# Norms on token columns, spread by products into PSUM, in a two-block kernel on one core

## What is computed

```python
def rmsnorm(x, g):
    xf = x.astype(jnp.float32)
    y = xf * lax.rsqrt(jnp.mean(xf * xf, axis=-1, keepdims=True) + NORM_EPS)
    return (y * g.astype(jnp.float32)).astype(x.dtype)

x = rmsnorm(x + y, final_g)                        # end of the first block
h = _rmsnorm(x, norm_mix_g) ; proj = h @ w_in      # start of the second
x = x + _mixer(...)
h = _rmsnorm(x, norm_ffn_g) ; u = h @ w_up         # FFN
x = x + _conv_ffn(...)
return _rmsnorm(x, norm_final_g)
```

## Time and profile before

| | us |
|---|---|
| median of 3 runs | 1647.12 (1646.19 to 1648.33) |
| the profiled execution | 1644.95 |
| its span | 1643.2 |
| TensorE busy | 1486.6 (90%) |
| VectorE busy | 1161.7 (71%) |
| ScalarE busy | 509.6 (31%) |
| POOL busy | 491.7 (30%) |

### The profile page before, as it was taken

How to read it: one execution, slowest core, us unless ns; L and a number is a source line. 1 busy time by engine, 2 the same in 40 slices (tenths; PEclk the granted TensorE clock), 3 DMA queues, 4 the chain that set the end, 5 groups by cost and what they waited for, 6 DMA issues and landing times.

```text
span 1643.2 us, 17617 instructions
## 1 busy us (share of the span) xinstructions
PE 1486.6 (90%) x7056; PEld 1171.9 (71%) x7056; DVE 1161.7 (71%) x1392; ACT 509.6 (31%) x670; POOL 491.7 (30%) x131
## 2 busy tenths in 40 slices
PE   6999778567998989999998888998997999999997
PEld 5778444357776868778887666776875888888885
DVE  3569988865485776679999999866245888886123
ACT  5432355411343433221221112332213333332221
POOL 0004011100143533234444233343342444344440
PEclk9999978875899999999999898999998999999999
DMA  6222000100022322223232222222332333332221
GB/s 184 81 85 77 1 1 1 51 1 28 26 89 91 103 79 84 69 78 94 86 103 77 77 77 77 77 77 77 103 98 56 96 84 102 103 103 96 77 84 51
DMA packets 163666, 123.44 MB, mean 75 GB/s; under 512 B 9115, under 2 KB 161474, under 8 KB 163586
## 3 DMA queue, kind: packets, MB, share of 16 engines
q1 hardware_dynamic: 163490, 122.19, 24.4%
q10 hardware_dynamic: 96, 0.13, 0.0%
HBM read 120.21 MB, written 2.10 MB: 74 GB/s over the span
## 4 chain that ended last, share of the span: by engine, by line
PE 63%; DVE 32%; ACT 2%; issue 2%; DMA 0%; SPq 0%; DVEq 0%; ACTq 0%
PE bank L399 17%; PE bank L400 17%; PE bank L401 17%; DVE conv_b L1929 10%; DVE op_hi L1472 2%; PE bank L552 2%; PE bank L359 2%; DVE score L1592 1%; DVE misc L1591 1%; DVE tmp L1483 1%; DVE x_res L1899 1%; PE bank L807 1%; PE bank L823 1%; DVE rs L1697 1%; DVE op_lo L1473 1%
## 5 line engine op out<-in xcount | busy, mean ns | idle before, releaser
L1008 POOL TENSOR_TENSOR w_lo<-w_raw,w_hi 128x2048 fp32r<-128x2048 f32 (+1 forms) x102 | 471.4, 4622 | 856.9 <-ACT w_hi L1055 828.8
L399 PE MATMUL bank<-op_hi,w_hi 128*128 128x512 f32 x1384 | 553.9, 400 | 50.8 <-issue 17.8
L400 PE MATMUL bank<-op_lo,w_hi 128*128 128x512 f32 x1384 | 546.8, 395 | 0.0
L401 PE MATMUL bank<-op_hi,w_lo 128*128 128x512 f32 x1384 | 546.1, 395 | 0.0
L399 PEld LDWEIGHTS bank<-op_hi,w_hi 128*128 128x128 f32 x1384 | 264.5, 191 | 117.2 <-issue 41.7
L400 PEld LDWEIGHTS bank<-op_lo,w_hi 128*128 128x128 f32 x1384 | 264.6, 191 | 57.2 <-issue 1.7
L401 PEld LDWEIGHTS bank<-op_hi,w_lo 128*128 128x128 f32 x1384 | 264.0, 191 | 57.5
L1055 ACT ACTIVATE w_hi<-w_raw 128x2048 fp32r<-128x2048 f32 (+1 forms) x111 | 210.4, 1895 | 263.6 <-PE bank L401 263.6
L1929 DVE SCALAR_TENSOR_TENSOR conv_b<-pad_b,par,conv_b 128x512 f32<-128x512 f32 x240 | 266.4, 1110 | 8.0
L2093 DVE TENSOR_TENSOR tmp<-tmp,conv_f 128x512 f32<-128x512 f32 x22 | 101.5, 4616 | 16.0 <-ACT tmp L1420 16.0
L1872 DVE TENSOR_TENSOR x_res<-bank,x_res 128x512 f32<-128x512 f32 x24 | 16.5, 688 | 123.6 <-PE bank L401 123.6
(11 more groups left out here) (362 smaller groups left out, 1864.5 us busy)
## 6 DMA issues: line engine op xcount, KB each, us to landing
w_raw<-in_w_in SPq DMA_DIRECT2D x31, 1024.0 KB, 5.0
w_raw<-in_w_up SPq DMA_DIRECT2D x44, 512.0 KB, 5.0
w_raw<-in_w_in SPq DMA_DIRECT2D x33, 512.0 KB, 5.1
w_raw<-in_w_kv SPq DMA_DIRECT2D x8, 1024.0 KB, 5.7
w_raw<-in_w_down SPq DMA_DIRECT2D x8, 1024.0 KB, 5.1
w_raw<-in_w_out SPq DMA_DIRECT2D x4, 1024.0 KB, 5.1
w_raw<-in_w_att_out SPq DMA_DIRECT2D x4, 1024.0 KB, 5.0
w_raw<-in_w_a_out SPq DMA_DIRECT2D x4, 1024.0 KB, 5.0
```

The source lines that it names most:

```text
L399: nc.tensor.matmul(b[:, 0:width], h, xh[:, x0 + k, 0:width], start=start and k == ks[0], stop=False)
L400: nc.tensor.matmul(b[:, 0:width], h, xl(x0 + k, width), start=False, stop=False)
L401: mm = nc.tensor.matmul(b[:, 0:width], l, xh[:, x0 + k, 0:width], start=False, stop=stop and k == ks[-1])
L1008: nc.gpsimd.tensor_tensor(w_lo[u % 2][:, 0:nk, :], w_raw[u % 2][:, 0:nk, :], w_hi[u % 2][:, 0:nk, :].bitcast(F32), ALU.subtract).then_inc( ...
```

## The change

The squares of chunks 0 to 5 are summed into chunk 0 on VectorE (`sum_squares`), five adds a key, where three pair sums were made. All products of the sums move behind the loop of their stage. `token_sums` makes the squares the stationary operand and a single column of ones the moving one, for each of the four blocks of 128 tokens and for chunk 0 (holding six), 6 and 7: the sums lie with tokens on partitions, in four columns of a bank. `token_variance` and the root then work on four columns (eight for the root between the blocks, which now takes both statistics at once). `spread` multiplies a column, broadcast to 128, with the identity, four times, and so puts the statistic of each token on all partitions of a whole bank. The scalings read it there: `r_y`, `r_mix`, `r_f`, `r_fin`. These banks are held until the norm is through: `rs_y` is freed by the last `mix_norm`, the others by `release`. Between the blocks the two spreads stand behind unit kT 0.

```diff
-            def sum_some(key, sq, first, last):
+            def token_sums(key, sq):
+                b = bank(key)
+                for n, c in enumerate((0, CH - 2, CH - 1)):
+                    if n:
                         pe.wait_ge(sem("sq_" + key), c + 1)
+                    else:
+                        pe.wait_ge(sem("summed_" + key), 1)
+                    for t in range(NT):
+                        mm = nc.tensor.matmul(b[:, t:t + 1], sq[:, c, t * P:t * P + P], ones[:, 0:1], start=n == 0 and t == 0,
+                                              stop=n == 2, skip_group_check=True)
+                done(mm, key)
+
+            def spread(key, col):
+                b = bank(key)
+                for t in range(NT):
+                    mm = nc.tensor.matmul(b[:, t * P:t * P + P], col[:, t:t + 1].to_broadcast([P, P]), ident[:, :], start=True, stop=True)
+                done(mm, key)
...
                 unit_tiles("wout", i, oh, ol, ready=None if i else "mix_ready", order=MIX_ORDER)
-                if i:
-                    sum_some("y", sq2, 2 * i - 2, 2 * i)
-                    sum_some("yg", sq_g, 2 * i - 2, 2 * i)
-            sum_some("y", sq2, CH - 2, CH)
-            sum_some("yg", sq_g, CH - 2, CH)
+            token_sums("y", sq2)
+            token_sums("yg", sq_g)
             for i in range(4):
                 unit_tiles("kT", i, memn_hi, plain(memn_lo), MEM)
+                if i == 0:
+                    pe.wait_ge(sem("tok_mix_ready"), 1)
+                    spread("rs_y", tok_rs)
+                    spread("rs_mix", tok_mix)
             unit_tiles("u", 0, oh, ol, ready="mixn_ready")
...
-                if i:
-                    sum_some("f", sq_f, 2 * i - 2, 2 * i)
-            sum_some("f", sq_f, CH - 2, CH)
+            token_sums("f", sq_f)
+            pe.wait_ge(sem("tok_f_ready"), 1)
+            spread("rs_f", tok_rs)
...
-                if i:
-                    sum_some("fin", sq3, 2 * i - 2, 2 * i)
-            sum_some("fin", sq3, CH - 2, CH)
+            token_sums("fin", sq3)
+            pe.wait_ge(sem("tok_fin_ready"), 1)
+            spread("rs_fin", tok_rs)
...
+            def sum_squares(key, sq, i):
+                dve.wait_ge(sem("sq_" + key), 2 * i + 2)
+                for c in (2 * i, 2 * i + 1):
+                    if c:
+                        ins = V.tensor_tensor(sq[:, 0, :], sq[:, 0, :], sq[:, c, :], ALU.add)
+                        if c == CH - 3:
+                            ins.then_inc(sem("summed_" + key), 1)
+                        else:
+                            link(ins)
+
+            def token_variance(key, scale, eps):
+                b = take(dve, key)
+                ins = V.tensor_scalar(tok_rs, b[:, 0:NT], scale, eps, ALU.mult, ALU.add)
+                evac(ins, key)
+                evacuated(dve, key)
+                return V.reciprocal(tok_rs, tok_rs)
...
-            variance("y", T, 1.0 / D, NORM_EPS)
-            evac(V.tensor_tensor(rs_mix, take(dve, "yg")[:, :], rs[:, :], ALU.mult), "yg")
+            link(token_variance("y", 1.0 / D, NORM_EPS))
+            b = take(dve, "yg")
+            evac(V.tensor_tensor(tok_mix, b[:, 0:NT], tok_rs, ALU.mult), "yg")
             evacuated(dve, "yg")
-            link(V.tensor_tensor(rs_mix, rs_mix, rs[:, :], ALU.mult))
-            link(V.tensor_scalar(rs_mix, rs_mix, 1.0 / D, EPS2, ALU.mult, ALU.add))
-            V.reciprocal(rs_mix, rs_mix).then_inc(sem("var_ready"), 1)
+            link(V.tensor_scalar(tok_mix, tok_mix, 1.0 / D, EPS2, ALU.mult, ALU.add))
+            V.reciprocal(tok_mix, tok_mix).then_inc(sem("tok_mix_var"), 1)
+            r_y, r_mix = take(dve, "rs_y"), take(dve, "rs_mix")
...
             def mix_norm(c):
                 x = x_res[:, c, :]
-                link(V.scalar_tensor_tensor(x, x, pcol("final_g", c), rs[:, :], ALU.mult, ALU.mult))
-                if c == 0:
-                    dve.wait_ge(sem("rs_ready"), roots[0])
-                scaled_chunk("norm_mix_g_2", c, rs_mix, "mixn")
+                ins = V.scalar_tensor_tensor(x, x, pcol("final_g", c), r_y[:, :], ALU.mult, ALU.mult)
+                if c < CH - 1:
+                    link(ins)
+                else:
+                    evac(ins, "rs_y")
+                    evacuated(dve, "rs_y")
+                ins = scaled_chunk("norm_mix_g_2", c, r_mix, "mixn")
                 if c:
                     lo_chunk(c - 1, "mixn")
...
             lo_chunk(CH - 1, "mixn")
+            release("rs_mix")
```

More of the change, by code:

```diff
@@ L239, in build @@
         pad_a = at("pad_a", R0 + 73728, [KA - 1 + T])
-        rs_mix = tmp[2][:, 0:T]
         u_sig = tmp[2][:, 0:T]
@@ L268, in build @@
         rs_mem = misc[:, 97:99]
+        tok_rs = misc[:, 99:103]
+        tok_mix = misc[:, 103:107]
         dec = misc[:, 65:81]
@@ L378, in next_unit @@
                 return u
-            def sum_some(key, sq, first, last):
[L383 to L388, removed]
-                        pe.wait_ge(sem("sq_" + key), c + 1)
-                        mm = nc.tensor.matmul(b[:, :], ones[:, :], sq[:, c, :], start=False, stop=c == CH - 1)
-                    done(mm, key)
+            def token_sums(key, sq):
+                b = bank(key)
+                for n, c in enumerate((0, CH - 2, CH - 1)):
+                    if n:
+                        pe.wait_ge(sem("sq_" + key), c + 1)
+                    else:
[9 more added lines that the diff above has]
+                done(mm, key)
             def tile(b, u, col, width, xh, xl, x0=0, start=True, stop=True, ks=None):
@@ L1057, in _, with root @@
             roots = [0]
[L1059 to L1063, removed]
+            def root(t=rs[:, :], done="rs_ready"):
+                if done == "rs_ready":
+                    roots[0] += 1
+                    act.wait_ge(sem("var_ready"), roots[0])
+                else:
+                    act.wait_ge(sem(done.replace("ready", "var")), 1)
+                A(t, t, ACT.Sqrt).then_inc(sem(done), 1)
             for t in range(NT):
@@ L1302, in _ @@
                     A(sq_g[:, c, :], x_res[:, c, :], ACT.Square, scale=pcol("final_g", c)).then_inc(sem("sq_yg"), 1)
-            root()
+            root(misc[:, 99:107], "tok_mix_ready")
             def hi_chunks(which, name):
@@ L1314, in _ @@
                 after_unit()
-                if i == 0:
-                    root(rs_mix)
-                else:
+                if i:
                     hi_chunks(((0, 1), (1, 3), (3, 5))[i - 1], "mixn")
@@ L1408, in _ @@
                     A(sq_f[:, c, :], x_res[:, c, :], ACT.Square).then_inc(sem("sq_f"), 1)
-            root()
+            root(tok_rs, "tok_f_ready")
             hi_chunks((0, CH), "ffn")
@@ L1427, in _ @@
                     A(sq3[:, c, :], x_res[:, c, :], ACT.Square).then_inc(sem("sq_fin"), 1)
-            root()
+            root(tok_rs, "tok_fin_ready")
             for g in range(2):
@@ L1481, in scaled_chunk, with release @@
             def scaled_chunk(gain, c, r, name):
-                V.scalar_tensor_tensor(tmp[c % 2][:, 0:T], x_res[:, c, :], pcol(gain, c), r[:, 0:T], ALU.mult, ALU.mult)\
-                    .then_inc(sem(name + "_scaled"), 1)
+                ins = V.scalar_tensor_tensor(tmp[c % 2][:, 0:T], x_res[:, c, :], pcol(gain, c), r[:, :], ALU.mult, ALU.mult)
+                ins.then_inc(sem(name + "_scaled"), 1)
+                return ins
+            def release(key):
+                dve.sem_inc(free[seq[key] % BANKS], 1)
             def lo_chunk(c, name):
@@ L1877, in pair_squares @@
                 V.tensor_tensor(sq[:, 2 * i, :], sq[:, 2 * i, :], sq[:, 2 * i + 1, :], ALU.add).then_inc(sem("paired_" + key), 1)
+            def sum_squares(key, sq, i):
[13 more added lines that the diff above has]
+                return V.reciprocal(tok_rs, tok_rs)
             for i in range(4):
                 if i:
-                    pair_squares("y", sq2, i - 1)
-                    pair_squares("yg", sq_g, i - 1)
+                    sum_squares("y", sq2, i - 1)
+                    sum_squares("yg", sq_g, i - 1)
                 residual("wout", i)
@@ L1886, in _ @@
                     evacuated(dve, ("wout", i, m))
-            variance("y", T, 1.0 / D, NORM_EPS)
-            evac(V.tensor_tensor(rs_mix, take(dve, "yg")[:, :], rs[:, :], ALU.mult), "yg")
+            link(token_variance("y", 1.0 / D, NORM_EPS))
+            b = take(dve, "yg")
+            evac(V.tensor_tensor(tok_mix, b[:, 0:NT], tok_rs, ALU.mult), "yg")
             evacuated(dve, "yg")
-            link(V.tensor_tensor(rs_mix, rs_mix, rs[:, :], ALU.mult))
-            link(V.tensor_scalar(rs_mix, rs_mix, 1.0 / D, EPS2, ALU.mult, ALU.add))
-            V.reciprocal(rs_mix, rs_mix).then_inc(sem("var_ready"), 1)
-            roots[0] += 1
+            link(V.tensor_scalar(tok_mix, tok_mix, 1.0 / D, EPS2, ALU.mult, ALU.add))
+            V.reciprocal(tok_mix, tok_mix).then_inc(sem("tok_mix_var"), 1)
```

(29 more changed lines are left out.)

## The result

The changed kernel takes 1652.62 us (median of 14 runs, 1648.88 to 1660.42) beside 1646.95 us for the kernel before (14 runs, 1643.02 to 1657.73). The ratio is 1.0034, 95% interval 1.0020 to 1.0049: slower by a third of a per cent. The forecast was 1.8 us faster, with a range up to 1652. In the profiled executions it is 1650.45 us (span 1648.7) against 1644.95 us (span 1643.2), +5.5.

What follows compares the result with a forecast made beforehand. At the three changed norms TensorE (63% busy) stands still for VectorE. Terms of +8.0 between the blocks, -5.5 ahead of the FFN and -4.3 at the end sum to -1.8 us: 1645.3 beside 1647.12, range 1638 to 1652.

Steps and rivals of the forecast that it cites:

- 0.12: Sums and spreads on TensorE: 0.12 us for each light fp32 pass, at full clock, bounds 0.06 and 0.23.
- the stand for the banks: Between the blocks: u 0 needs the banks holding rs_y and rs_mix, so TensorE stands idle 15 us, until 591.1.
- Norm start: Between the blocks: VectorE's norm may begin at 556.3 instead of 559.9 us.
- The norm itself: Between the blocks: PSUM-operand instructions never stretched, op_lo stalled two or three times, norm over at 590.9, 3.3 us earlier.
- 44 units: Evidence for unstretched PSUM forms: 742 to 753 ns in 66 cases, in a stage where POOL splits 44 units.
- Rival (a): Between the blocks: banks don't block, u 0 runs beside the norm, -3.3 instead of +8.0, 1634.0 us; chance 0.05.
- rival (c): Between the blocks: clock stays at 1.2 GHz for all of u 0, +7.3, sum +5.5, 1652.6 us; chance 0.07.
- Between the blocks in all: From wout to q2: +8.0 us, u 0 ending at 604.3 against 596.33; bounds +5.7 and +8.8.
- Ahead of the FFN and at the end: Two later norms: -5.5 us ahead of the FFN (first up product -4.7), -4.3 us at the end.
- the clock's 0.8: Ahead of the FFN: half the idle time wins back 0.8 of the 2.5 us that slow products cost.
- The sum: Whole kernel: +8.0 - 5.5 - 4.3 = -1.8 us, 1645.3 beside the median of 1647.12.
- Rival (b): All 96 light passes on the path cost 0.23 us: +10.6, in sum +8.8, 1655.9 us; chance 0.08.

Runs made afterwards that it cites:

- e2_wide_sums: Changed kernel with all token-sum passes streaming 128 columns of ones instead of one; 1643.96 us, ratio to the kernel before 0.9982.
- e5_kt_first: Changed kernel with kT 0 ahead of the sums of y and yg and the spreads behind kT 1; 1638.23 us, ratio to the kernel before 0.9923.
- e1_free_banks: Changed kernel with the bank numbers of rs_y and rs_mix swapped with those of kT 1; 1639.89 us, ratio to the kernel before 0.9966.
- e8_sums_32: Changed kernel with 32 columns of ones in the token sums instead of one; 1650.97 us, ratio to the kernel before 1.0009.
- e7_free_wide: Changed kernel with rs_y and rs_mix swapping banks with kT 1, and 128 columns of ones in the sums; 1635.36 us, ratio to the kernel before 0.9916.

## Why the prediction was wrong

It failed in one step, the price of a pass. The term "0.12" was mis-sized for the passes between the blocks, and the products behind them were slowed with it. The mechanism of the rest, the stand for the banks above all, was as stated. By the medians it is +5.7 us for -1.8. Of the 7.5 us between, 4.8 lie in the touched stages (+3.0 for -1.8): between the blocks 4.5 for that step and 0.8 for a wait overlooked, less 1.2 in the norm, and 0.7 ahead of the FFN, where the clock was down as well. The other 2.6 lie ahead of wout, where the prediction had no term and where nothing was changed.

- **"I take 0.12, since the engine comes from dense work each time."** The size at full clock was right: 0.119 us (0.95 over 8) and 0.120 (2.88 over 24). The reason was not. Between the blocks 24 of the passes cost 0.219 us each (5.26 over 24), at a granted clock of 0.50, and kT 0 behind them 7.3 us instead of 5.8. The sum counted 7.7 us from wout's end to kT 0; it was 10.5. With 128 columns (e2_wide_sums) it is 7.5 and 5.8. The clock fell behind such passes even where dense products stood right ahead of them, with no idle time between (e5_kt_first).
- **The Trainium skill**, page "TensorE: Matmul & The Clock Gate", section "LDWEIGHTS (loading the stationary operand)", takes the time of a load from its columns alone (columns over 1.2, in ns: 107 for 128). The trace has 0.119 us a pass at full clock, for 1 column and (2.84 over 24) for 128, so the moving columns did not set the pace; but at 1.2 GHz a pass is 0.219, nearly twice that.
- **Norm start.** It was to begin behind the first spread, 556.3; it begins at 563.90 less the 2.4 us by which all is later, 561.5. Besides some 4.5 us of the slower passes and kT 0, VectorE takes both statistics (`take` of rs_y and of rs_mix) before its first instruction, so it waits for 16 passes, not 8: 0.8 us that the code showed.
- **The norm itself.** PSUM forms at 0.75, three op_lo stalls (4.66, 4.30, 3.44): as stated. (The prediction's "44 units" beside L2087 is a miscount: POOL has 21 passes there. The 742 to 753 ns stand.) From its start to u 0 33.6 us, forecast 34.8.
- **The stand.** Forecast 15 us idle for a bank, measured 15.3, and e1_free_banks shows the cause. Rival (a) is out. u 0 took 13.4 us, forecast 13.2, with 0.54 of the clock for 5.6 us; rival (c) is out.
- **Between the blocks in all** (wout included): forecast +8.0, measured +12.0. The 4.0 are the clock and the 0.8, less 1.2 in the norm.
- **Ahead of the FFN and at the end.** wo2 and the norm: forecast -4.7, measured -4.0; the spread ran at 1.2 GHz (2.08 for 8 passes), which stood among the bounds. The last paragraph of the prediction counts the 4.7 from wo2's last product, but 1.7 of it were wo2's own; from there it is 1.6 measured (11.95 to 10.38) for 3.0. From the last sum to the first chunk it is 2.9 us ahead of the FFN and 2.0 at the end, forecast 2.0 and 2.1. up, down and the final norm: forecast -5.1 with the clock's 0.8, measured -5.0. wout: -3.4, measured -3.6.
- **The sum.** The touched stages gave +3.0 for -1.8. The other 2.6 us of the profiled difference lie ahead of wout, in instructions that the change leaves alone. With +3.0 alone the time would have been 1650, inside the forecast's range.
- **Rival (b)** had the mechanism and the wrong extent: it put all 96 passes at 0.23, for 10.6 us. Some 42 ran at 1.2 GHz (the 24 of yg, the 8 of the FFN's spread, and by their starts 6 of y and 4 of the FFN's sums), and half of kT 0's time with them; after against e2_wide_sums it is 5.2 us between the blocks and 1.3 ahead of the FFN. It deserved more than 0.08.

## What to carry to other kernels

A run of TensorE passes with few columns is not to be costed by its columns, nor at the clock of the dense work ahead of it: at full clock a pass took 0.12 us here with 1, 64 or 128 columns, and the light passes with the products behind them ran at 1.2 GHz for 3.4 us (e5_kt_first) to 10.2 us (after). Before an accumulation result is parked in a bank that goes round, count who asks for that bank next, and number it so that nobody does before its release. Where the engine must wait for a last operand, put independent dense work there first: that order, which also moved the held banks apart from u 0, turned touched stages 3.0 us over before into 14.1 us under it (0.9%), and 14.9 with wider passes.

## What the runs showed of the hardware

- **A gapless run of light passes came with a fallen clock.** Passes with 1 or 32 columns behind 128x128 weights, with TensorE busy throughout in the timeline, ran at a granted clock of 0.50 behind the wait (after, e8_sums_32); the same passes with 128 columns ran at 1.00 behind the same wait (e2_wide_sums). More arithmetic was faster, by 2.4 us over 24 passes. The busy column did not tell the two apart. It is no rule for every light pass: behind dense work 48 of them ran at 1.00 and the clock fell only then (e5_kt_first), and the 24 at the end of after took 2.88 us at 1.00.
- **The part ahead of wout, the same instructions in every kernel, took 489.6 to 501.8 us.** Some 9 of the 11.6 us between before (the second shortest of ten) and e7_free_wide (the longest) are one stretch of small products in the scan, here in both:

```profile
416.00:458.00 42.00, 37.90 (x280) 27.02 (x279) 20.60 (x34) 14.55 (x24) 8.35 (x2) 0.88 0.08 26
```

```profile
416.00:458.00 42.00, 38.80 (x257) 28.71 (x257) 17.27 (x27) 9.95 (x15) 4.51 (x1) 0.66 0.08 26
```

The granted clock is 0.88 in the one and 0.66 in the other for the same stretch of time, and the second gets through fewer instructions (24 of ScalarE's against 15). Runs of one kernel fall in two groups about as far apart, for before 1644 to 1648 and 1652 to 1657 us beside the last four experiments, the second with a lower mean clock (0.942 to 0.945 and 0.937 to 0.941); that the scan makes them is likely, but only one execution of a kernel was profiled. What decides the clock at that place stays open. The 2.6 us between before and after do not come from it: in after the products that start at 331.00 in before start 2.9 us later already.

```profile
333.86 3.65 PE L612 MATMUL bank<-tok_v,g_k 128*128 128x64 f32 x16 [11.50 <-DVE g_k L1742]
```

From 49 to 54 us the clock is 1.00 in before and 0.66 in after, with TensorE busy throughout in both. The spread of the untouched part is larger than the effect under study, and a reason to compare stages where single profiles are compared.
- **The price of an op_lo stall hangs on when it meets POOL's pass** (3.44 to 4.66 us; each of the three ended 0.55 us behind the pass that it met), while the instructions with a PSUM operand kept to 0.75 us beside the same passes. The Trainium skill, page "SBUF — State Buffer", section "Who interferes with whom", says so of the two kinds, and the trace agrees.
